# Start of a hybrid encoder step: identity first, token-wise squares for the first norm, two transfers moved back

## The reference, cut to what matters

```
x = x + mixer(rms_norm(x, norm_mix[i]))
x = x + (relu(rms_norm(x, norm_mlp[i]) @ w_up) ** 2) @ w_down
rms_norm(x, g) = x * rsqrt(mean(x * x, axis=-1) + 1e-6) * g
```

## Time and profile before

| what | value |
| --- | --- |
| time, median of 3 runs | 3022.16 us (3018.03 to 3022.17) |
| time of the profiled execution | 3018.97 us |
| span of the profiled execution | 3016.9 us |
| TensorE matmul busy | 2865.7 us, 95% of the span |
| VectorE busy | 42% |
| ScalarE busy | 29% |
| GpSimd busy | 9% |
| mean granted TensorE clock | 0.971 of full speed |

### The profile page before, as it was taken

The page is one execution under the profiler, slowest core; times in us unless marked ns, Lnnn a source line. Parts: engine busy times, 40 slices in busy tenths (PEclk is TensorE's granted clock), DMA queues, the critical chain, the costliest instruction groups (busy, mean ns, idle before and its releaser), DMA issues.

```text
span 3016.9 us, 49528 instructions
## 1 busy us (share of the span) xinstructions
PE 2865.7 (95%) x21191; PEld 2776.5 (92%) x21191; DVE 1274.5 (42%) x1612; ACT 860.5 (29%) x891; POOL 273.9 (9%) x238
## 2 busy tenths in 40 slices
PE   6999999999996799999998689999999999999998
PEld 5987999999996799999998679999999878999997
DVE  3346543333435343334346654333343365433333
ACT  3136432222211232223223233122231264322222
POOL 5000100000104200000102620000010000000001
PEclk8999999999997899999999779999999999999999
DMA  3210232222221222222221012222222101322221
GB/s 122 87 65 1 80 109 82 84 84 84 84 84 42 56 84 84 84 84 70 85 70 64 1 42 84 84 84 84 81 96 77 53 32 60 113 84 84 84 84 46
DMA packets 205445, 223.38 MB, mean 74 GB/s; under 512 B 3734, under 2 KB 200416, under 8 KB 205312
## 3 DMA queue, kind: packets, MB, share of 16 engines
q1 hardware_dynamic: 200336, 203.70, 21.1%
q0 software_dynamic: 4976, 17.74, 1.8%
HBM read 208.56 MB, written 12.86 MB: 73 GB/s over the span
## 4 chain that ended last, share of the span: by engine, by line
PE 77%; issue 15%; DVE 3%; ACT 2%; POOL 2%; DMA 1%; POOLq 0%; DVEq 0%; ACTq 0%
PE bank L340 67%; PE bank L446 4%; PE bank L420 2%; PE bank L589 1%; POOL big L1420 1%; ACT big L795 1%; PE bank L477 1%; DMA out<-mixs 1%; PE bank L413 0%; PE bank L634 0%; DVE mixs L1128 0%; PE bank L631 0%; PE bank L643 0%; DVE stg L1221 0%; DVE stg L1248 0%
## 5 line engine op out<-in xcount | busy, mean ns | idle before, releaser
L340 PE MATMUL bank<-ahi,whi 128*128 128x288 f32 x3584 | 770.1, 297 | 7.0 <-DVE alo L1003 6.5
L340 PE MATMUL bank<-alo,whi 128*128 128x288 f32 x3584 | 767.4, 296 | 0.0
L340 PE MATMUL bank<-ahi,wlo 128*128 128x288 f32 x3584 | 767.1, 296 | 0.0
L682 ACT ACTIVATE whi<-raw 128x2048 fp32r<-128x2048 f32 x191 | 365.0, 1911 | 897.5 <-PE bank L340 877.6
L340 PE MATMUL bank<-hhi,whi 128*128 128x288 f32 x2560 | 556.6, 299 | 54.2 <-DVE hlo L1138 39.7
L340 PEld LDWEIGHTS bank<-ahi,whi 128*128 128x128 f32 x3584 | 578.5, 189 | 9.9 <-DVE wlo L976 7.4
L340 PEld LDWEIGHTS bank<-alo,whi 128*128 128x128 f32 x3584 | 578.2, 189 | 0.0
L340 PEld LDWEIGHTS bank<-ahi,wlo 128*128 128x128 f32 x3584 | 577.9, 189 | 0.0
L340 PE MATMUL bank<-hlo,whi 128*128 128x288 f32 x2560 | 553.2, 298 | 0.0
L340 PE MATMUL bank<-hhi,wlo 128*128 128x288 f32 x2560 | 553.2, 298 | 0.0
L976 DVE TENSOR_TENSOR wlo<-raw,whi 128x2048 fp32r<-128x2048 f32 x192 | 440.2, 2293 | 261.5 <-ACT whi L682 259.5
(11 more groups left out here) (250 smaller groups left out, 1787.4 us busy)
## 6 DMA issues: line engine op xcount, KB each, us to landing
raw<-in_mlp_w_up SPq DMA_DIRECT2D x64, 1024.0 KB, 5.3
raw<-in_mlp_w_down SPq DMA_DIRECT2D x64, 1024.0 KB, 5.1
raw<-in_sb_w_qkv SPq DMA_DIRECT2D x24, 1024.0 KB, 5.2
raw<-in_conv_w_in SPq DMA_DIRECT2D x12, 1024.0 KB, 5.2
raw<-in_gla_w_in SPq DMA_DIRECT2D x12, 1024.0 KB, 5.3
raw<-in_sb_w_o SPq DMA_DIRECT2D x8, 1024.0 KB, 5.3
out<-mixs POOLq DMA_DIRECT2D x3, 2048.0 KB, 7.7
out<-big POOLq DMA_DIRECT2D x2, 2048.0 KB, 8.4
```

The lines of the kernel that those rows point to most:

```text
L340: mm = pe.matmul(acc[h][:, 0:HALF], w[:, u, k, m * P:(m + 1) * P], a[:, k, h * HALF:(h + 1) * HALF], start=(k == 0 and w is whi and a is a ...
L682: act.activation(whi[:, 1 - u], raw[:, 1 - u], ACT.Copy).then_inc(w_hi, 1)
```

## The change

`ident` gets a semaphore of its own, `ident_ready`, and is made on POOL ahead of its DMA issues. TensorE's transposes wait for that alone; the wait for the other five constants moves into `sum_squares(0)`.

For the first norm only, the squares are taken from x as it arrives: ACT squares tile t (frames on the partitions, 1024 features along the free side) as soon as `x_in[t]` has come, and its accumulator output gives one number for each frame, `x_sq[:, t]`. The squared values themselves go to `stg`, where nobody reads them. POOL turns each column into a 128x128 diagonal block of `ssq` by multiplying `ident` with it, so that the same `negones` matmul over partitions gives the same sums. `add_squares(0)` and ACT's eight `squared(0, j)` go.

On ACT four tiles are squared ahead of the copies from PSUM, the fifth behind them; `whi` of slab 0 is now made ahead of the copy of `vec` and no longer behind the wait for DVE's fifth copy.

On POOL `rank_raw` and `CK` are issued after the diagonal blocks, still ahead of the `lmask` work.

```diff
 (TensorE)
@@ def sum_squares(i):
                 pe.wait_ge(ssq_add, 9 * (i + 1))
+                if i == 0:
+                    pe.wait_ge(const_ready, CONSTS)
@@
-            pe.wait_ge(const_ready, CONSTS)
+            pe.wait_ge(ident_ready, 1)
 (ScalarE)
+            def token_squares(t):
+                n = P if t < 4 else TS
+                act.wait_ge(x_in[t], 16)
+                act.activation(stg[0:n, 0:D], flat(0, 9)[0:n, t * D:(t + 1) * D], ACT.Square,
+                               accum_out=x_sq[0:n, t:t + 1]).then_inc(x_squared, 1)
+                act.wait_ge(x_squared, t + 1)
+
+            act.sem_inc(sq_ready, 8)
+            for t in range(4):
+                token_squares(t)
             for c in range(1, KC, 2):
                 evacuate(c, X[:, c, 0:TP], bank[c][:, :])
+            token_squares(4)
+            act.wait_ge(slab_in[0], 16)
+            act.activation(whi[:, 0], raw[:, 0], ACT.Copy).then_inc(w_hi, 1)
             evacuate(TB_VEC, vec[:], bank[1][:, 0:V_ROWS])
             act.wait_ge(ev_v, 5)
             act.wait_ge(ev_a, 5)
-            act.wait_ge(slab_in[0], 16)
-            act.activation(whi[:, 0], raw[:, 0], ACT.Copy).then_inc(w_hi, 1)
             for j in range(KC):
                 gained(0, j, V_MIX)
-            for j in range(KC):
-                act.wait_ge(ssq_add, j + 1)
-                squared(0, j)
 (GpSimd: made() and the two lines of ident now stand ahead of the seven small transfers)
-            pool.dma_start(rank_raw[:], ...).then_inc(rank_in, 16)
-            pool.dma_start(CK, ...).then_inc(ck_in, 16)
@@
             pool.tensor_copy(sums[:, 0, :], tri[:]).then_inc(const_ready, 1)
+            pool.wait_ge(const_ready, 1)
             pool.tensor_scalar(sums[:, 1, :], negones[:], 1 / TRI, None, ALU.mult).then_inc(const_ready, 1)
@@
-            pool.wait_ge(const_ready, 5)
+            pool.wait_ge(ident_ready, 1)
             pool.tensor_copy(identb[:], ident[:]).then_inc(const_ready, 1)
@@
-            add_squares(0)
+            def token_sums():
+                made(pool.memset(ssq, 0.0))
+                for t in range(NT):
+                    n = P if t < 4 else TS
+                    pool.wait_ge(x_squared, t + 1)
+                    pool.tensor_scalar(ssq[0:n, t * P:t * P + n], ident[0:n, 0:n], x_sq[0:n, t:t + 1], None,
+                                       ALU.mult).then_inc(ssq_add, 1)
+                pool.sem_inc(ssq_add, 4)
+
+            token_sums()
+            pool.dma_start(rank_raw[:], ...).then_inc(rank_in, 16)
+            pool.dma_start(CK, ...).then_inc(ck_in, 16)
@@
-CONSTS = 6
+CONSTS = 5
```

More of the change, by code:

```diff
@@ L110, in trunk @@
         lmask = sb("lmask", [P, 8, P], U8)
+        x_sq = sb("x_sq", [P, NT], F32)
         rank_raw = sb("rank_raw", [P, KC, 16], F32)
@@ L154, in trunk @@
         vec_in, const_ready, pool_step = sem("vec_in"), sem("const_ready"), sem("pool_step")
+        ident_ready, x_squared = sem("ident_ready"), sem("x_squared")
         tp_ready, ev_v, ev_a = sem("tp_ready"), sem("ev_v"), sem("ev_a")
@@ L1372, in _, with made @@
         def _(pool):
+            steps = [0]
+            def made(ins):
+                ins.then_inc(pool_step, 1)
+                steps[0] += 1
+                pool.wait_ge(pool_step, steps[0])
+            made(pool.memset(ident[:], 0.0))
+            pool.affine_select(ident[:], ident[:], [[-1, P]], ALU.not_equal, 1.0, base=0,
+                               channel_multiplier=1).then_inc(ident_ready, 1)
             row = 0
@@ L1383, in _ @@
                 row += n
-            pool.dma_start(rank_raw[:], gla_w_in[0].rearrange("(k p) c -> p k c", p=P)[:, :, 3 * D:3 * D + 16])\
-                .then_inc(rank_in, 16)
-            pool.dma_start(CK, cache_sb_k[0, 0].rearrange("(j p) h d -> p j (h d)", p=P)).then_inc(ck_in, 16)
-            steps = [0]
-            def made(ins):
-                ins.then_inc(pool_step, 1)
-                steps[0] += 1
-                pool.wait_ge(pool_step, steps[0])
-            made(pool.memset(ident[:], 0.0))
-            pool.affine_select(ident[:], ident[:], [[-1, P]], ALU.not_equal, 1.0, base=0,
-                               channel_multiplier=1).then_inc(const_ready, 1)
             pool.memset(negones[:], -TRI).then_inc(const_ready, 1)
@@ L1420, in add_squares @@
                     pool.tensor_tensor(ssq, ssq, sq_x, ALU.add).then_inc(ssq_add, 1)
-            add_squares(0)
+            def token_sums():
[7 more added lines that the diff above has]
+            token_sums()
+            pool.dma_start(rank_raw[:], gla_w_in[0].rearrange("(k p) c -> p k c", p=P)[:, :, 3 * D:3 * D + 16])                .then_inc(rank_in, 16)
+            pool.dma_start(CK, cache_sb_k[0, 0].rearrange("(j p) h d -> p j (h d)", p=P)).then_inc(ck_in, 16)
             lm = stg[:, 4096:4096 + P]
```

## The result

The change gives 2981.06 us as the median of four runs (2962.68 to 2988.49), against 3021.33 for the kernel before in the same session: a ratio of 0.9865, 95% interval 0.9837 to 0.9893. The gain is 40 us, or 32 to 49 by the interval. The profiled execution took 2988.49 us, with a span of 2986.5, 30.4 us less than before.

A forecast was written before the change was run, and what follows sets the result against it. TensorE, busy 95% of the span, was taken as the bound, with gains only in its start-up waits: 6.1 + 12.1 + 2.0 - 0.1 = 20.1 us, giving 2998.9 us profiled and a forecast of 3000, range 2993 to 3007.

The forecast's parts named there:

- first projection: Start of layer 0's projections: first matmul at 19.0 us and not 25.12, a gain of 6.1 us.
- wait for the sum of squares: Ahead of the first norm's sum: TensorE's 12.1 us wait for POOL's last square disappears, the largest term.
- the sum at 28: First norm's sum on TensorE: starts near 28 us at the upper clock; running there without the stall gives 2.0 us.
- the second readout: DVE's readout of the second projection chunk: near 35.7 us, some 20 us before 55.84.
- `whi` at 13.9: ACT's making of `whi` for slab 0: begins at about 13.9 us, with slab 0 landing at 13.7 and not 16.65.
- rival 1: At the start: slab 0 lands no sooner because something other than `CK` sets it; gain 17.3 us, time 3003; chance 0.12.
- The new wait at the third chunk: Behind the second chunk: TensorE waits 0.1 us for the first chunk's readout, a loss.
- rival 2: Around the first norm: GpSimd's masks slow DVE's `alo` and six steps, costing 3.3 us; time 3003.5; chance 0.09.
- The step that failed: Everything behind the second chunk: instructions follow as before, so the 20.1 us gain stays whole to the end.
- Rival 3: Behind the start: the gain is given back by a hidden layer 0 wait or lower clock; about 3020 us; chance 0.05.
- The 2% left for a gain beyond 22.5 us: Whole kernel: a chance of 0.02 for a gain above the forecast's 18.5 to 22.5 us.
- the 46 behind the sum at 387.26: First norm's restart: 46 more matmuls at 0.133 us take 6.1 us, part of 7.7 us to the second readout.

The follow-up runs named there:

- e4: The changed kernel with only `rank_raw` and `CK` issued where the kernel before issues them; 2985.54 us, ratio 0.9881.
- e10: The changed kernel with TensorE waiting, ahead of the fourth chunk of each of eight stretches, for its own third chunk; 3002.68 us, ratio 0.9945.
- e6: The changed kernel with `x_sq` declared behind the operands, so that these have the addresses of the kernel before; 2998.16 us.
- e18: e6 plus the restart wait of e10 and a 32-column extra matmul at block k = 4 of the fourth chunk; 2966.25 us, ratio 0.9815.
- e17: The kernel before plus e10's restart wait and a 32-column extra matmul, nothing of the change; rest behind the start 2902.6 us, 47.6 less than before's.
- e1: The changed kernel run again unchanged; 2991.55 us over six runs, ratio 0.9899.
- e15_restart_nudge: The changed kernel plus e10's restart wait and a 32-column extra matmul at block k = 4 of the fourth chunk; 2966.87 us, ratio 0.9819.
- e7: e6 with the activations alone moved by 32 bytes; mean matmul interval 133.3 ns, total time not given in the text.
- e8: e6 with the weights moved by 32 bytes and the activations by 64; mean matmul interval 133.3 ns, total time not given in the text.

## Why the prediction was wrong

**The start was right, term by term.** Forecast against measured: first projection 19.0, 18.63; wait for the sum of squares gone, none seen; the sum at 28, 27.35, with its four matmuls in 1.13 us and so at the upper clock; the second readout 20.1 us earlier, 20.8. The single figures hold too: a 1024-wide square 1.06 us, 1.06; its accumulator between nothing and 0.3 us, and it is a short instruction of its own of 0.19; the fifth square's end at 13.4 to 14.0, 13.46; `whi` at 13.9, 13.49. With the transfers left in place `whi` stands at 17.65 (e4), so the two transfers did hold slab 0 back (`CK` 1 MB, `rank_raw` 64 KB, moved together), and rival 1 falls. The diagonal block of the fifth tile ends at 13.98, 13 us before it is wanted.

**Terms a little off.** The new wait at the third chunk is 0.26 us on TensorE, on top of a sum that reached the first readout 6.85 us after its start: DVE's step at L1024 took 0.85 us where it took 0.48 before, and the next 0.86 for 0.76, beside a select. That is rival 2 in small, 0.5 us and not 3.3. The eight `alo` took 0.84 us each (0.837 to 0.842), where the median before was 0.815. The first of them ran beside three selects that took 3.29 us, 1.1 each, where the median before was 0.4. So here it was GpSimd that lost the time and not `alo`. The rule of the Trainium skill, "SBUF — State Buffer", section "Who interferes with whom", says that DVE and GpSimd shut each other out of a port pair that they share; the trace agrees that they hold each other up, and shows the loss on DVE's side that rival 2 feared only at the two steps above, 0.5 us in all.

**The step that failed** is "From then on every instruction should follow as before, so the gain stays whole to the end." The instructions do follow as before, but not at the same pace. Two things were taken for nothing: that the pace behind each norm depends on how the stream restarts there, and that a 32-byte tile, which costs no time, moves every operand of every projection. e10 (slow pace throughout: 2999.6 us without its restarts) comes out at the forecast once the pace is held, and e6 (old addresses: a gain of 20.1) comes out at it by terms that partly cancel. In the profile after, the 20.5 us of the third chunk became 17 with Q0's lost pace, 20.5 by layer 2, and 30 with M3 at the fast pace (10 us); the runs below it must owe the rest to further fast stretches, which were not profiled. Up to the third chunk the forecast held; what came behind it did not. Rival 3 had the place right, a difference that comes later, but the wrong sign and reasons: I named waits and the clock, and looked for neither pace nor addresses. The 2% left for a gain beyond 22.5 us had no mechanism at all.

**The row that could have warned** was there: a matmul took "9.00 / 71 = 0.13 us" in the earlier trace rows, but 0.133 was the figure that I used for the 46 behind the sum at 387.26. Both came from the trace of before, 0.127 and 0.133, and I took the difference for rounding. (71 counts matmuls cut by the window's edges too; by their starts those of 51 to 60 us are 130.0 ns apart, the fast pace, and those behind 387.26 are at the slow one.) Over the some 15000 matmuls of the eight stretches 3.3 ns each are 50 us, more than twice the change.

**What stays open.** Why the address changes the odds; why e18 does not restart like e17; whether the chip has a part in the odds, since of the kernels in the experiments only before ran on more than one; and the last 1 to 4 us of the rest, which lie in the lengths of the stretches at the lower clock in layer 2. A single run of before in the second session took 2997.05 us, where its others took 3008 and more; it was not profiled, and whether its pace was fast is inferred. How often each stretch is fast was seen only in the profiled runs, one for each kernel.

## What to carry to other kernels

In a kernel bound by one engine, count that engine's instructions in equal windows at the same clock, before pricing anything else: a busy share of 100% can hide two paces, and the difference can outweigh the edit. A measured gain of an edit that adds a tile or shifts the restart of a long stream holds its own effect and that of the pace; run the edit with the old addresses, and the old kernel with the new ones, before believing either. And the start of this kernel could be forecast from one profile to about a microsecond, which is also what it varies by from run to run (the third chunk starts at 35.12 in after, at 33.93 in e1): the chain, the waits, and who is next in line.

The best versions here are e18_after_old_addr_nudge and e15_restart_nudge, the change with the restart and the extra matmul: 2966.25 and 2966.87 us, ratios 0.9815 and 0.9819, 15 us below the median of after and 55 below before. The intervals of e15 (0.9794 to 0.9843) and after (0.9837 to 0.9893) just touch; against the ten runs of after together (median 2987.4) the difference is 20 us.

## What the runs showed of the hardware that was not expected

- TensorE runs the same stream (128x128 weights, 288 columns, granted clock 1.00, a weight load beside every matmul) at 130.0 or 133.3 ns a matmul, 387 or 377 in 50 us; the pace holds for up to 3000 matmuls, through every change of chunk and slab. Where weights and activations are shifted against each other by 32 bytes (e7, e8), the intervals are 135 and 132 ns in turn, again 133.3 in the mean, and no stretch is fast.
- One extra matmul of 32 columns, 27 ns, put behind the 140 ns step of the slow pattern, turned it into the fast one in 28 of 28 cases, and elsewhere in the pattern in none of 6. Extra matmuls of 64 to 256 columns put into the fast pattern turned it slow in 6 of 6.
- An accumulator output on ACT is a second instruction of 0.18 to 0.20 us behind the square.
